# Decoder trunk of two layers on one Trainium2 core: chunked handover at the norms, split weight tiles ahead, router turned round, nested rounds

## The reference, cut to what matters

```python
for i in range(DEPTH):                                   # DEPTH = 2
    sh1, sc1, g1, sh2, sc2, g2 = split(silu(c) @ w_ada[i] + b_ada[i])   # per sequence
    h = rmsnorm(x, g_norm_mix[i]) * (1 + sc1) + sh1
    y = nsa_mixer(h, caches) if i % 2 == 0 else conv_mixer(h, state)
    x = x + g1 * y
    h = rmsnorm(x, g_norm_ffn[i]) * (1 + sc2) + sh2
    f = swiglu(h) if i % 2 == 0 else moe(h)              # top 2 of 8 experts
    x = x + g2 * f
return rmsnorm(x, g_norm_final)

def conv_mixer(h, state):                                # short gated convolution, width 3
    bg, cg, v = split(h @ w_in, 3);  u = cg * v
    ue = concat([state or zeros, u])
    return (bg * (w0*ue[:-2] + w1*ue[1:-1] + w2*ue[2:])) @ w_out
def moe(h):
    logits = h @ w_router + b_router
    top_v, top_i = top_k(logits, 2);  w = softmax(top_v)
    return sum(w[e] * swiglu_e(h) for the two chosen experts)
```

## Time and profile before

| What | Value |
|---|---|
| Median of 3 runs | 2190.1 us (2185.01 to 2194.22) |
| Profiled execution | 2183.5 us, span 2181.7 us |
| Busy share of the span | PE 91%, PEld 72%, DVE 70%, ACT 54%, POOL 1% |
| Chain that ended last | PE 79%, DVE 8%, issue 4%, ACT 2%, DMA 2%, SPq 2% |
| HBM | 533.32 MB read, 250 GB/s over the span |

### The profile page before, as it was taken

One profiled execution on the slowest core, in us unless ns is written; L12 is line 12 of the kernel. 1 busy time (PEld: TensorE's weight loads), 2 busy tenths in 40 slices (PEclk: granted clock), 3 DMA queues, 4 the chain that ended last, 5 costly groups with the idle time before them and its releaser, 6 DMA issues.

```text
span 2181.7 us, 31104 instructions
## 1 busy us (share of the span) xinstructions
PE 1986.3 (91%) x10717; PEld 1578.4 (72%) x10717; DVE 1524.2 (70%) x2040; ACT 1180.3 (54%) x1338; POOL 15.0 (1%) x26
## 2 busy tenths in 40 slices
PE   5998899888688999978779999999999999999993
PEld 3655534655468999978658888887888888888882
DVE  6666620586525444355679898998989899898984
ACT  4555400244213333242258777887877787877771
POOL 0000000100000000000000000000000000000000
PEclk9999999899899999989879999999999999999996
DMA  9888713401877554434149999999999999999970
GB/s 298 274 295 298 270 62 97 130 1 40 256 208 283 163 172 164 165 116 137 60 165 343 351 340 353 354 356 347 340 345 346 346 357 363 340 343 346 346 267 24
DMA packets 262793, 537.67 MB, mean 246 GB/s; under 512 B 14876, under 2 KB 56068, under 8 KB 262438
## 3 DMA queue, kind: packets, MB, share of 16 engines
q1 hardware_dynamic: 258514, 520.34, 68.2%
q0 software_dynamic: 1984, 13.45, 1.8%
q10 hardware_dynamic: 2196, 2.61, 0.4%
HBM read 533.32 MB, written 11.35 MB: 250 GB/s over the span
## 4 chain that ended last, share of the span: by engine, by line
PE 79%; DVE 8%; issue 4%; ACT 2%; DMA 2%; SPq 2%; DVEq 0%; ACTq 0%; POOL 0%; PEldq 0%
PE ps L2127 14%; PE ps L1539 13%; PE ps L2092 9%; PE ps L2094 9%; PE ps L2093 9%; PE ps L1933 5%; PE ps L1935 5%; PE ps L1934 5%; DVE alo L906 2%; PE ps L2040 2%; DMA ring<-in_w_ada 1%; SPq L535 1%; PE ps L2076 1%; PE ps L1592 1%; PE ps L1824 1%
## 5 line engine op out<-in xcount | busy, mean ns | idle before, releaser
L1481 DVE TENSOR_TENSOR wlo<-ring,whi 128x1024 fp32r<-128x1024 f32 x672 | 797.0, 1221 | 84.6 <-ACT whi L857 58.9
L857 ACT ACTIVATE whi<-ring 128x1024 fp32r<-128x1024 f32 x672 | 706.7, 1061 | 211.1 <-PE ps L2094 130.9
L2092 PE MATMUL ps<-whi,XTh 128*128 128x512 f32 x896 | 355.2, 396 | 4.4 <-DVE wlo L1481 4.4
L2094 PE MATMUL ps<-whi,XTl 128*128 128x512 f32 x896 | 350.7, 391 | 0.0
L2093 PE MATMUL ps<-wlo,XTh 128*128 128x512 f32 x896 | 350.2, 391 | 0.0
L2092 PEld LDWEIGHTS ps<-whi,XTh 128*128 128x128 f32 x896 | 168.9, 188 | 37.4 <-issue 4.8
L2094 PEld LDWEIGHTS ps<-whi,XTl 128*128 128x128 f32 x896 | 168.7, 188 | 36.5
L1300 DVE TENSOR_TENSOR flo<-ring,fhi 128x2048 fp32r<-128x2048 f32 x42 | 96.3, 2292 | 137.4 <-ACT fhi L647 137.4
L2093 PEld LDWEIGHTS ps<-wlo,XTh 128*128 128x128 f32 x896 | 169.0, 189 | 32.1
L647 ACT ACTIVATE fhi<-ring 128x2048 fp32r<-128x2048 f32 x42 | 80.4, 1914 | 174.2 <-PE ps L1935 174.2
L906 DVE TENSOR_TENSOR alo<-ring,ahi 128x2048 fp32r<-128x2048 f32 x48 | 109.4, 2280 | 59.8 <-ACT ahi L640 59.6
(11 more groups left out here) (357 smaller groups left out, 3060.2 us busy)
## 6 DMA issues: line engine op xcount, KB each, us to landing
ring<-in_w_moe_gu SPq DMA_DIRECT2D x224, 1024.0 KB, 6.8
ring<-in_w_moe_down SPq DMA_DIRECT2D x112, 1024.0 KB, 7.1
ring<-in_w_ada SPq DMA_DIRECT2D x48, 1024.0 KB, 8.8
ring<-in_w_ff_gu SPq DMA_DIRECT2D x28, 1024.0 KB, 5.3
ring<-in_cache_cmp_kv SPq DMA_DIRECT2D x128, 128.0 KB, 2.7
ring<-in_cache_sel_kv SPq DMA_DIRECT2D x128, 128.0 KB, 2.4
ring<-in_w_ff_down SPq DMA_DIRECT2D x14, 1024.0 KB, 5.0
ring<-in_w_conv_in SPq DMA_DIRECT2D x12, 1024.0 KB, 5.1
```

What stands on the lines that cost most here:

```text
L857: a.activation(whi[:, i % SPLIT, c0:c0 + HALF], ring[:, (T_MOE + i) % RING, c0:c0 + HALF], ACT.Copy).then_inc(s_split_hi, 1)
L1481: v.tensor_tensor(wlo[:, i % SPLIT, c0:c0 + HALF], ring[:, (T_MOE + i) % RING, c0:c0 + HALF], whi[:, i % SPLIT, c0:c0 + HALF].bitcast(F32) ...
L2092: pe.matmul(out, XTh[:, kc, :], hi, start=kc == 0, stop=False)
L2094: ins = pe.matmul(out, XTl[:, kc, :], hi, start=False, stop=kc == 7)
```

## The change

- Norms 1 and 2: DVE handles a chunk at a time. xhat, sample scale, sample shift of chunk c, then the split of chunk c−1 (`norm_split`, new).
- PE's norm matmuls move ahead. Norm 1: one after each of W_O's blocks from the third on, the last two behind. Norm 2: four at the FFN's tile 40. Norm 3: four in the middle of the last conv tile. The residual and the squares of chunks 0 to 3 of norm 2 move to FFN tiles 38 and 39.
- First weight tiles: ACT copies FFN tiles 0 and 1 ahead of norm 1's squares, DVE subtracts both ahead of W_O's residual. Conv tile 0 is split ahead of the second half of norm 2 (its buffer moved to where the FFN's buffers lie), conv tile 1 behind it.
- A one-column root (`warm`) stands ahead of each deviation, behind the squares; the table load goes with it.
- Router: the router's columns are the weights, the tokens move; the logits come out as 8 rows and are turned back by three small transposes, with the first eight token transposes of `to_tokens` put ahead.
- Routing: `hNl` on DVE goes from behind the count to behind the logits' shift; clearing `yacc` goes behind the matrices; the count is loaded before the experts.
- Rounds 1 and 2 are nested: one jump at the end where there were two.

```diff
 # buffers: chi/clo behind convrows and a gap
+        convrows = conv_sb("convrows", [18, 2048], F32)
+        conv_sb("conv_gap", [128, 1120], F32)
         chi = conv_sb("chi", [128, SPLIT_F, SLOT])
...
 # ACT
-            def squares(n):
-                for c in range(DC):
+            def squares(n, cs=range(DC)):
+                for c in cs:
...
             def deviation(n):
+                a.activation(warm, C("eps"), ACT.Sqrt)
                 a.wait_ge(s_ss_done, n + 1)
...
+            a.wait_ge(s_group_pv, 4)
+            ffn_hi(0)
+            ffn_hi(1)
             norm(1)
-            for i in range(1, TILES_F):
+            for i in range(2, TILES_F):
                 ffn_hi(i)
+                if i == 39:
+                    squares(2, range(4))
...
-            norm(2)
+            conv_hi(0)
+            squares(2, range(4, DC))
+            deviation(2)
+            scale_shift(2)
+            conv_hi(1)
             a.dma_start(strow, A["state_conv"][0]...).then_inc(s_state_in, 16)
...
 # DVE
+            def norm_split(n, xh, xl):
+                lay, k = n // 2, 3 * (n % 2)
+                v.wait_ge(s_std_ready, n + 1)
+                v.reciprocal(rstd[:], std[:]).then_inc(s_rstd_ready, 1)
+                v.wait_ge(s_rstd_ready, n + 1)
+                for c in range(DC + 1):
+                    if c < DC:
+                        v.tensor_tensor(nT[:, c, :], xT[:, c, :], rstd[:], ALU.mult).then_inc(s_xhat_ready, 1)
+                        v.wait_ge(s_xhat_ready, 8 * n + c + 1)
...
+                        link(v.tensor_tensor(nS, nS, modT[:, lay, k + 1, c, 1:9]..., ALU.mult))
+                        ins = v.tensor_tensor(hS, nS, modT[:, lay, k, c, 1:9]..., ALU.add)
+                        ins.then_inc(s_h_chunk if c < 7 else s_h_sample, 1)
+                    if c:
+                        d = c - 1
+                        v.wait_ge(s_h_prompt, 8 * n + d + 1)
...
+                        link(v.tensor_copy(xh[:, d, :], hT[:, d, :]))
+                        v.tensor_tensor(xl[:, d, :], hT[:, d, :], xh[:, d, :].bitcast(F32), ALU.subtract).then_inc(s_h_split, 1)
...
-            residual(0, 2, from_wo)
-            norm(1)
...
             ffn_lo(0)
-            v.wait_ge(s_h_sample, 2)
-            for c in range(DC):
...
+            ffn_lo(1)
+            residual(0, 2, from_wo)
+            norm_split(1, hTh, hTl)
+            for i in range(2, TILES_F):
                 ffn_lo(i)
+                if i == 38:
+                    residual(0, 5, from_dn, range(4))
...
             conv_lo(0)
+            residual(0, 5, from_dn, range(4, DC))
+            norm_split(2, cTh, cTl)
             conv_lo(1)
...
 # PE: norm(n, cs) as squares(n, cs); in dense(), after each block of W_O
+                    if nd[done] >= 3:
+                        norm(1, (nd[done] - 3,))
...
+                    if t == 40:
+                        norm(2, range(4))
...
-            norm(2)
-            h_ready(2)
-
+            norm(2, range(4, DC))
+            pe.wait_ge(s_std_ready, 3)
             pe.wait_ge(s_state_in, 16)
...
+                    if i == 15 and q == 2:
+                        norm(3, range(4))
...
-            for t, (t0, m) in enumerate(TOK):
-                for kc in range(DC):
-                    ins = mm(ps[0:m, 7, 8 * t:8 * t + 8], hT[:, kc, t0:t0 + m], wr[:, kc, :], kc, DC)
-            ins.then_inc(s_logits_done, 1)
+            for kc in range(DC):
+                pe.wait_ge(s_h_prompt, 24 + kc + 1)
+                ins = mm(ps[0:8, 7, 0:NTOK], wr[:, kc, :], hT[:, kc, :], kc, DC)
+            ins.then_inc(s_lgT_done, 1)
...
+            to_tokens(hT, (0, 1))
+            pe.wait_ge(s_lgT_taken, 1)
+            for t, (t0, m) in enumerate(TOK):
+                ins = pe.transpose(ps[0:m, 7, 288 + 8 * t:296 + 8 * t], lgT[:, t0:t0 + m], ident[0:8, 0:8])
+            ins.then_inc(s_logits_done, 1)
+            to_tokens(hT, range(2, 6))
...
 # each of SP, ACT, DVE, PE (SP loads the count behind experts(0))
+            c_ = pe.value_load(cnti[0:1, 0:1], min_val=0, max_val=NTOK)
             experts(0)
-            c_ = pe.value_load(cnti[0:1, 0:1], min_val=0, max_val=NTOK)
-            for rnd in (1, 2):
-                with pe.If(c_ > SLOTS_E * rnd):
-                    experts(rnd)
+            with pe.If(c_ > SLOTS_E):
+                experts(1)
+                with pe.If(c_ > SLOTS_E * 2):
+                    experts(2)
```

More of the change, by code:

```diff
@@ L267, in trunk @@
         peb = small[:, 44:46]
+        warm = small[:, 60:61]
+        lgT = actM[0:8, 0, 0:NTOK]
         mx4, sm4 = smp[:, 296:300], smp[:, 300:304]
@@ L680, in norm @@
                 squares(n)
[L681 to L685, removed]
                 deviation(n)
@@ L821, in _ @@
             norm(3)
+            a.wait_ge(s_lgT_done, 1)
+            a.activation(lgT, ps[0:8, 7, 0:NTOK], ACT.Copy).then_inc(s_lgT_taken, 1)
+            for i in range(6):
+                a.wait_ge(s_rows_done, i + 1)
+                t, h = i // 2, i % 2
+                m = TOK[t][1]
+                a.activation(hNh[0:m, t, 512 * h:512 * h + 512], ps[0:m, i, :], ACT.Copy).then_inc(s_rows_hi, 1)
             a.wait_ge(s_logits_shift, 1)
@@ L883, in experts @@
                 y_hi(1)
-            experts(0)
             a.wait_ge(s_count_ready, 1)
             c = a.value_load(cnti[0:1, 0:1], min_val=0, max_val=NTOK)
-            for rnd in (1, 2):
-                with a.If(c > SLOTS_E * rnd):
-                    experts(rnd)
+            experts(0)
+            with a.If(c > SLOTS_E):
+                experts(1)
+                with a.If(c > SLOTS_E * 2):
+                    experts(2)
             norm(4)
@@ L1408, in _ @@
             v.tensor_tensor(lg[:], lg[:], mE[:, 0:3].unsqueeze(2).to_broadcast([128, 3, 8]), ALU.subtract).then_inc(s_logits_shift, 1)
+            for i in range(6):
+                v.wait_ge(s_rows_hi, i + 1)
+                t, h = i // 2, i % 2
+                m = TOK[t][1]
+                v.tensor_tensor(hNl[0:m, t, 512 * h:512 * h + 512], ps[0:m, i, :],
+                                hNh[0:m, t, 512 * h:512 * h + 512].bitcast(F32), ALU.subtract).then_inc(s_rows_taken, 1)
             v.wait_ge(s_logits_exp, 1)
@@ L1415, in _ @@
             v.wait_ge(s_pos_done, 1)
-            v.tensor_copy(pos, ps[:, 7, 32:56].rearrange("p (t e) -> p t e", t=3))
-            link(v.tensor_reduce(mE[:, 12:13], ps[:, 7, 56:64], AX, ALU.max))
+            v.tensor_copy(pos, ps[:, 7, 320:344].rearrange("p (t e) -> p t e", t=3))
+            link(v.tensor_reduce(mE[:, 12:13], ps[:, 7, 344:352], AX, ALU.max))
             v.tensor_copy(cnti[:], mE[0:1, 12:13]).then_inc(s_count_ready, 1)
-            for i in range(6):
-                v.wait_ge(s_rows_hi, i + 1)
-                t, h = i // 2, i % 2
-                m = TOK[t][1]
-                v.tensor_tensor(hNl[0:m, t, 512 * h:512 * h + 512], ps[0:m, i, :],
-                                hNh[0:m, t, 512 * h:512 * h + 512].bitcast(F32), ALU.subtract).then_inc(s_rows_taken, 1)
-            link(v.memset(yacc[:], 0.0))
             def matrices(rnd, e0, chain):
@@ L1473, in experts @@
                 matrices(rnd, 0, base)
+                if rnd == 0:
+                    v.memset(yacc[:], 0.0)
                 gathered_lo(B)
@@ L1559, in _, with norm @@
             pe.wait_ge(s_x_ready, 8)
-            def norm(n):
-                for c in range(DC):
+            def norm(n, cs=range(DC)):
+                for c in cs:
                     if n and c == 0:
```

87 lines of the change are left out of this document (42 added, 45 removed).

## The result

The changed kernel takes 2195.2 us in the median of 12 runs, against 2187.2 of the kernel before on the same chips: ratio 1.0038 (95% interval 1.0025 to 1.0051), 8.0 us slower. The forecast was 2194 by a sum of +4.3, added to 2190.1, the median of three runs; the range held it. The two profiled executions are 2183.5 and 2195.1, their spans 2181.7 and 2193.3, 11.6 apart.

| From | to | before | after | difference | forecast |
|---|---|---|---|---|---|
| start | W_O's first matmul | 612.0 | 615.8 | +3.7 | 0 (untouched) |
| W_O's first matmul | FFN's first | 48.1 | 52.6 | +4.5 | +4.2 (A) |
| FFN's first | FFN's last, end | 268.6 | 277.0 | +8.4 | +2.0 (part of B) |
| FFN's last, end | first xhat of norm 2 | 9.1 | 7.4 | −1.7 | −1.6 (rest of B) |
| first xhat | conv's first matmul | 7.7 | 13.7 | +5.9 | +5.8 (C) |

The account below looks back on a forecast made before the run. PE was taken to bound the kernel, never idle inside the FFN, with time to be had only at stage borders. Terms at the borders summed to +4.3 us, added to the 2190.1 median: 2194 us, range 2179 to 2205.

Parts of the forecast that it names:

- A: W_O and norm 1: chunked split saves time, but PE waits some 6.6 us for chunk 0's square; +4.2 us.
- B: Norm 2: four matmuls ahead of FFN tile 40 cost 2.0, conv tile 0's copy leaves the path; +0.4 us.
- C: Conv's start: state rows' DMA behind chunked scale and shift, first matmul 13.6 behind first xhat; +5.8 us.
- R4: FFN: a weight tile held behind the window copy starves PE; +6.0 us, +8.5 with later landing; chance 0.13.
- The bound without a stall: W_O and norm 1: if PE did not wait in W_O, the change there would give −3.7 us.
- D: Norm 3: four norm matmuls ahead of the conv's end, with no copy leaving the path; +1.9 us.
- E: Router: small-column matmuls and transposes take 8.3 us where 48 records took 7.92; +0.4 us.
- F: Routing: logits to first gather takes 13.2 us instead of 16.5; −3.3 us.
- G: The end: one jump, at the longer price of 4.6, replaces a load and two jumps of 8.5; −3.8 us.
- The prediction's other sum: The end: by the page-fetch rule the remaining jump could cost like the first, 2.87; sum 1.7 us lower.
- H: Norm 4: the table load of 1.28 goes beside the sixteen matmul records; −1.3 us.
- the 3.9 by that page: Norms 1, 2 and 4: a set switch of about 2.7 us at the warm instruction would add 3.9 us in all.

Follow-up runs that it names:

- Two experiments: Changed kernel with norm 1's matmuls behind W_O again: 2180.46 us; changed kernel with residuals of earlier chunks ahead of the two early splits: 2185.45 us.
- The MoE part alone: Kernel before with only the change's router, routing, count load and nested rounds: 2177.8 us against 2188.45, ratio 0.9958.

## Why the prediction was right, and what inside it was wrong

The sign and the place of most terms came out; the size was +8.0 for +4.3, short mainly by one term that stood outside the sum, the held tile (R4).

- *A.* Held: +4.5 for +4.2, with a wait of 6.2 for 6.6. Two experiments, from PE's side and from DVE's and ACT's, remove it. The restart behind the wait was nearer to the dear bound: in the timeline block 4's residual comes 7.0 behind PE's restart (636.09 to 643.08), the later ones 4.4 apart, so 2.6 for 1.8. The bound without a stall, −3.7, does not follow from the prediction's own terms (4.2 − 6.6 − 1.8 = −4.2); the two experiments came to −4.7 and −5.0.
- *B, D.* At the FFN's end the four matmuls took 1.94, the forecast 2.0; norm 2's other part −1.7 for −1.6. D seems to have cost 0.4 instead of 1.9, because the conv in the profiled execution of before was itself some 2 us long, with a clock of 0.93 over it instead of 0.95; against the three other profiles with that code (121.8 to 122.4) it is +2.1 to +2.7.
- *C.* Held: +5.9 for +5.8, first matmul at 13.7 for 13.6. The bound of +1.9 more did not come: the DMA was issued at 963.46, ahead of the copy of tile 1 at 963.86.
- *E, F.* Held: logits to gather 13.1 for 13.2; the router 8.1 for 8.3.
- *G.* The mechanism held, the size was off: the jump left over costs 2.95, not the longer price of 4.58. The Trainium skill (Runtime: NRT & Kernel Launch, Instruction fetch mechanics) has a taken branch out of the window fetch its target's page. The prediction's other sum, with the jump left over at the price of the first, came nearer. Why the second cost 4.58 stays open.
- *H.* Held: −1.6 for −1.3. The load now follows the last square (2170.97) and no longer the sixteen records, which end at 2172.1, just ahead of its own end; it still stands in the chain. The MoE part alone, with quicker records but the load behind them, gained 0.1 there in its one profile; how much of the 1.6 is the load's place and how much the quicker records and transposes is not shown.
- *The load ahead.* The Trainium skill (ScalarE: Activation LUTs, What ACT_TABLE_LOAD costs) has a drain of 1.4 with the load. In the changed kernel the load at 661.90 takes 1.28 and the one-column root starts at 663.19, so nothing shows between them, and the 3.9 by that page didn't come.
- *R4.* Here the prediction failed: it priced the held tile at +6.0, gave it 0.13 and left it out of the sum, on the ground that "tiles issued just ahead of the copy's first packets escape". Not all do: the tile issued at 661.1, 0.6 ahead of the copy's issue at 661.70, took 47.4; one issued 1.0 ahead did escape, with 6.4. The other ground, that "two splits ahead free nothing in the ring early", failed too: tile 6 was issued 7.3 ahead of the FFN's first matmul instead of 0.8, so just ahead of the copy and no longer behind it. The FFN paid 4.7 of waiting and some 1.3 of restart (twelve matmuls behind it come 0.24 apart instead of 0.13), 6.4 by the table: the size was right, the chance was wrong. The rows were there: before, the held tile was taken 0.5 us after landing, and the change brought the FFN's start 6.9 us nearer to the copy (6.7 behind its issue instead of 13.6; the prediction had 7.2). The 2.2 of slack that the prediction had itself worked out cannot stand that; this was arithmetic, not a rival. In that slack 6.21 us a tile is misread: the 261 us of the earlier trace rows hold 1965 records, 41 tiles of 48 and not 42, and a tile takes 6.36; with 1.4 instead of 2.1 for the cold tile PE came to tile 6 at 699.7, for 699.5.

That the total was close is largely luck: of the sum, +6.4 was left out, while −1.7 at the end and −1.5 in the conv were not foreseen, and the base, the median of three runs, lay 2.9 above that of twelve (2190.1, 2187.2). The sum was 3.7 short, the base 2.9 high.

## What to carry to other kernels

Ahead of an edit that brings a stage nearer to a bulk transfer, work out when the last tile that the transfer holds is needed; here a copy in packets of 65 KB made the tiles of a stream in packets of 2 KB wait for its end, and cutting it into smaller rows or spread pieces took the wait away. A matmul put between others in order waits for all that its input stands behind on the other engines: look at what was put ahead of its producer in the same change. Work moved in among full tiles of the bounding engine cost its whole length here (1.9 to 2.4 for four matmuls) and bought nothing, since it hadn't been last before. The base of a sum should be as well measured as what is added to it.

## What the runs showed of the hardware

With packets of 65 KB beside packets of 2 KB the copy's queue got 6.24 MB of 7.20 in 30 us; with rows of 1 KB, 3.94 of 7.93. The Trainium skill (DMA: Bandwidth & Descriptors, Queues, rings and completion order) says that an engine goes round its queues packet by packet; the nearly equal packet counts in the second case (1982 and 2014) agree. In the first they are 96 and 487, five to one, which that rule alone does not give; whether what the trace calls a packet is what the page calls one, no run here shows. A tile issued 0.6 or 0.1 us ahead of the large copy was held for the copy's whole length (47.4 and 49.5), one issued 1.0 ahead was not (6.4). The conv came at a granted clock of 0.93 or 0.95 with the same code, which goes with 2 us in that stage between executions (124.1, and 121.8 to 122.4).
